# A transformer kernel on one core: order of norms, evictions and first units at three places, and a layer norm split five to three

## What is computed

```
h = h + rms_norm(first_block_output, post_norm_gain)
# layer 1, gated MLP
u, v, z = split(rms_norm(h, a_pre_g) @ w_in, 3)        # 3 x 2048 columns
u = gelu(u);  v = layer_norm(gelu(v), ln_g, ln_b)
s = causal(w_s) mixed over the 128 tokens of a chunk of v, + b_s
y = (u * s * silu(z)) @ w_out
h = h + rms_norm(y, a_post_g)
# layer 2, windowed attention
k, v = rms_norm(h, kv_norm_g) @ w_k, ... @ w_v         # 256 columns each
q, z = rms_norm(h, b_pre_g) @ b_w_in ...
```

## Time and profile before

| | |
|---|---|
| median of 3 runs | 2735.89 us (2731.44 to 2737.82) |
| profiled execution, its own time | 2731.15 us |
| its span in the profile | 2729.3 us |
| PE busy | 2634.8 us, 97% of the span |
| DVE, ACT, POOL busy | 1319.5, 819.5, 1039.3 us |
| mean granted TensorE clock | 0.991 |

### The profile page before, as it was taken

How to read it: one execution, slowest core, us unless ns; L and a number is a source line. 1 busy time by engine, 2 the same in 40 slices (tenths; PEclk the granted TensorE clock), 3 DMA queues, 4 the chain that set the end, 5 groups by cost and what they waited for, 6 DMA issues and landing times.

```text
span 2729.3 us, 42831 instructions
## 1 busy us (share of the span) xinstructions
PE 2634.8 (97%) x17184; PEld 2150.5 (79%) x17184; DVE 1319.5 (48%) x2475; ACT 819.5 (30%) x1623; POOL 1039.3 (38%) x1310
## 2 busy tenths in 40 slices
PE   6999999999999999999899899999999998999999
PEld 5778787777877878787787788788887887877777
DVE  4225343445857667585533533543435006477643
ACT  3344343536214131321213311211113103455531
POOL 2322332323233132321367433344444555444452
PEclk9999999999999999999999999999999998999999
DMA  4111111111101010111432211111111113111122
GB/s 134 41 38 47 51 40 51 47 39 46 49 24 59 21 47 27 34 48 63 158 124 77 78 39 47 39 47 47 42 44 47 47 51 96 39 47 40 47 109 85
DMA packets 203989, 153.92 MB, mean 56 GB/s; under 512 B 5264, under 2 KB 183824, under 8 KB 203280
## 3 DMA queue, kind: packets, MB, share of 16 engines
q1 hardware_dynamic: 186256, 106.44, 13.2%
q10 hardware_dynamic: 17536, 44.74, 4.4%
HBM read 128.10 MB, written 23.07 MB: 55 GB/s over the span
## 4 chain that ended last, share of the span: by engine, by line
PE 78%; DVE 14%; ACT 6%; issue 1%; DMA 1%; POOL 1%; DVEq 0%; ACTq 0%; SPq 0%; POOLq 0%
PE gemm L621 19%; PE gemm L623 19%; PE gemm L622 19%; ACT prob L2377 3%; DVE neg_logits L1804 2%; DVE prob L1819 2%; PE scores L672 1%; PE weighted L699 1%; PE scores L869 1%; PE probs_t L684 1%; PE probs_t L866 1%; PE scores L1044 1%; PE scores L858 1%; PE probs_t L887 1%; DVE stats L1808 1%
## 5 line engine op out<-in xcount | busy, mean ns | idle before, releaser
L582 POOL CAST w_hi<-w_raw 128x512 fp32r<-128x512 f32 x346 | 240.5, 695 | 1570.1 <-PE gemm L623 1504.0
L621 PE MATMUL gemm<-h_hi,w_hi 128*128 128x512 f32 x1904 | 779.3, 409 | 10.9 <-ACT q_t L2021 7.6
L623 PE MATMUL gemm<-h_hi,w_lo 128*128 128x512 f32 x1904 | 746.9, 392 | 0.0
L622 PE MATMUL gemm<-h_lo,w_hi 128*128 128x512 f32 x1904 | 745.4, 391 | 0.0
L584 POOL TENSOR_TENSOR w_lo<-w_raw,w_hi 128x256 fp32r<-128x256 f32 x692 | 590.7, 854 | 54.7
L621 PEld LDWEIGHTS gemm<-h_hi,w_hi 128*128 128x128 f32 x1904 | 360.0, 189 | 90.4 <-issue 22.5
L623 PEld LDWEIGHTS gemm<-h_hi,w_lo 128*128 128x128 f32 x1904 | 358.9, 189 | 78.3
L622 PEld LDWEIGHTS gemm<-h_lo,w_hi 128*128 128x128 f32 x1904 | 360.3, 189 | 65.2 <-issue 1.9
L1586 DVE TENSOR_TENSOR scaled_product<-gemm,norm_rstd 128x512 f32<-128x512 f32 x108 | 74.7, 691 | 310.7 <-PE gemm L623 308.6
L1284 DVE CUSTOM_DVE_ANT_0 neg_logits<-scores,bias_tile 128x128 f32<-128x128 f32 (+1 forms) x192 | 67.6, 352 | 148.7 <-PE scores L672 142.9
L621 PE MATMUL gemm<-xn_hi,w_hi 128*128 128x512 f32 x288 | 116.9, 406 | 2.6 <-DVE xn_lo L1732 2.2
(11 more groups left out here) (511 smaller groups left out, 4528.7 us busy)
## 6 DMA issues: line engine op xcount, KB each, us to landing
w_raw<-in_w_in SPq DMA_DIRECT2D x73, 512.0 KB, 3.9
w_raw<-in_a_w_in SPq DMA_DIRECT2D x48, 512.0 KB, 3.8
gates_scratch<-o_f ACTq DMA_DIRECT2D x32, 256.0 KB, 2.0
merge_gates<-gates_scratch ACTq DMA_DIRECT2D x4, 2048.0 KB, 15.0
w_raw<-in_a_w_out SPq DMA_DIRECT2D x16, 512.0 KB, 3.8
w_raw<-in_b_w_in SPq DMA_DIRECT2D x16, 512.0 KB, 3.9
x_rows<-in_x SPq DMA_DIRECT2D x8, 512.0 KB, 8.3
w_raw<-in_w_out SPq DMA_DIRECT2D x8, 512.0 KB, 3.9
```

Source lines behind the costliest of these rows:

```text
L582: Q(pool.tensor_copy(weight_part(u, 0, ks), raw[:, s, ks, :]))
L621: pe.matmul(dst, w_high, hi(k, h), start=first, stop=False)
L622: pe.matmul(dst, w_high, lo(k, h), start=False, stop=False)
L623: m = pe.matmul(dst, w_low, hi(k, h), start=False, stop=last)
```

## The change

At place A, `v_pair` runs the first three steps of V0 before the first of V1, and then goes on in pairs. The sum for the first block's second half moves from after step 2 to after step 4, and the spread of that norm from the end of the pair to after step 5. `v_next` puts its sum one step earlier for half 0 and two steps earlier (before all of V2) for half 1, and the spread one step earlier. DVE takes two evictions one tile earlier, and the statistics of group 1 (four `bn_stats`) go behind the evictions of group 2. The transposition of `w_s` comes one V unit later.

At place B, DVE normalises five chunks and ACT three. DVE empties the first half of Z0 after its second chunk, and the second half after its fifth. PE computes the first half of U1 before it waits for the layer norm.

At place C, the second norm of the residual is worked out one tile earlier and spread one step earlier. The first norm of half 1 comes one tile later on DVE and ACT. The first half of V1 is emptied one tile earlier. K0 of half 1 runs its first three steps before K1's first.

```diff
             def v_pair(h):
-                for k in range(KT):
+                for i in range(2):
+                    for k in range(3):
+                        h2_ready(k, h)
+                        gemm_step(U_V + i, h, k, *H2)
+                for k in range(3, KT):
                     h2_ready(k, h)
                     for i in range(2):
                         gemm_step(U_V + i, h, k, *H2)
-                    if (h, k) == (0, 2):
+                    if (h, k) == (0, 4):
                         sum_half(1, O_SECOND[-1], ADD_OUT[1, O_SECOND[-2]], SQ_OUT[1, O_SECOND[-1]])
-                if h == 0:
-                    spread_cols(4, 8)
+                    if (h, k) == (0, 5):
+                        spread_cols(4, 8)
             def v_next(h):
                 for k in range(KT):
+                    if k == 1 - h:
+                        sum_half(h, KT - 1, ADD_X2[h, KT - 2], SQ_X2[h, KT - 1])
                     gemm_step(U_V + 2, h, k, *H2)
-                    if k == 1:
-                        sum_half(h, KT - 1, ADD_X2[h, KT - 2], SQ_X2[h, KT - 1])
-                    if k == 4:
+                    if k == 3:
                         spread_cols(4 * h, 4 * h + 4)
...
-                if g == 5:
+                if g == 6:
                     pe.wait_ge(E("ws_in"), 32)
...
                 for h in range(2):
-                    if i or h:
+                    if (i, h) not in ((0, 0), (1, 0)):
                         gemm_half(U_UZ + 2 * i, h, *H2)
                 for h in range(2):
                     gemm_half(U_UZ + 2 * i + 1, h, *H2)
-                pe.wait_ge(E("v_normed"), 4)
-                pe.wait_ge(E("v_normed_act"), 4)
+                if i == 0:
+                    gemm_half(U_UZ + 2, 0, *H2)
+                pe.wait_ge(E("v_normed"), 5)
+                pe.wait_ge(E("v_normed_act"), 3)
...
-                if k == 6:
+                if k == 5:
                     spread_cols(4, 8)
...
+            def second_ready(k, h):
                 pe.wait_ge(E("low_part"), PART["xn"] + KT + k + 1)
+            for j in range(2):
+                for k in range(3):
+                    second_ready(k, 1)
+                    gemm_step(U_KV + j, 1, k, *XN)
+            for k in range(3, KT):
+                second_ready(k, 1)
                 for j in range(2):
                     gemm_step(U_KV + j, 1, k, *XN)
...
                 if k == 4:
-                    v_scaled(1, 0)
-                if k == 5:
                     v_scaled(1, 1)
+                if k == 5:
                     v_rows_in(0)
...
             for b in range(2):
                 v_scaled(2, b)
+            v_stats(1)
             for b in range(2):
                 v_scaled(3, b)
...
-            for n in range(4):
+            for n in range(5):
                 V(v.tensor_scalar(vln[:, n, :], vln[:, n, :], mv[:, n, 0:1], stat[:, 336 + n:337 + n], ALU.subtract, ALU.mult), E("v_normed"))
-            evict_z(0)
+                if n == 1:
+                    scaled(U_UZ + 1, 0, scaled_g[:, 0, :])
+            scaled(U_UZ + 1, 1, scaled_g[:, 1, :])
...
-                if k == 6:
+                if k == 5:
                     rstd(4, 8, MB)
...
-                if k == 0:
+                if k == 1:
                     rstd(0, 4)
-                if k == 1:
+                if k == 2:
                     rstd_in_sbuf(3)
                     for j in range(2):
                         key_part(j, 0)
                 if k == 3:
                     value_part(0, 0)
-                if k == 5:
+                if k == 4:
                     value_part(1, 0)
...
-                    for n in range(4, 8):
+                    for n in range(5, 8):
                         A(a.activation(vln[:, n, :], vln[:, n, :], ACT.Identity, bias=stat[:, 344 + n:345 + n], scale=stat[:, 336 + n:337 + n]), E("v_normed_act"))
...
-                if k == 7:
+                if k == 6:
                     root(4, 8)
...
-                if k == 1:
+                if k == 2:
                     root(0, 4, (0, 4))
```

More of the change, by code:

```diff
@@ L1631, in v_rows_in, with v_stats @@
                       E("vln_rows"))
+                if g != 1:
+                    v_stats(g)
+            def v_stats(g):
                 if g in (1, 3) or g % 4 == 3:
@@ L1635, in v_rows_in @@
                         V(v.bn_stats(bn[:, n, s, :], vln[:, n, HALF * s:HALF * s + HALF]))
-                if g == 4:
+                if g == 5:
                     dve.wait_ge(E("ws_tr"), 1)
@@ L1656, in _ @@
                     v_scaled(0, 1)
+                if k == 3:
+                    v_scaled(1, 0)
                 if k == 4:
-                    v_scaled(1, 0)
+                    v_scaled(1, 1)
                 if k == 5:
-                    v_scaled(1, 1)
                     v_rows_in(0)
```

## The result

The changed kernel took 2713.66 us in the median of four runs (2712.95 to 2719.32), the kernel before 2735.22 us (2731.44 to 2737.82). The ratio is 0.9925, interval 0.9911 to 0.9939. The profiled execution has a span of 2711.1 us against 2729.3, so 18.2 us are gone in it; the forecast had 20.5.

The account below looks back on a forecast made before the run. PE bounds the kernel, so only its waits and slow-clock stretches at three places count. Gains of 8.4 + 5.2 + 6.9 = 20.5 us from the 2735.89 us median give 2715 us, range 2708 to 2724.

Parts of the forecast that it names:

- The three waits named: PE's waits: 6.4 us for DVE's evictions at A, 3.7 us for ACT at B, 5.6 us for a V half's eviction at C.
- Place A, 8.4 us: Place A, V3's end and its transposition: 9.3 us earlier, taken as 8.4 us, with ends at 5.5 and 10.5 us.
- the mild slowing of POOL: Place A: POOL's split of V2 loses 1 us beside DVE's work, not the 2.5 us of the strict port rule.
- I add 2 us: Place A, from V2's start: 2 us added to PE's 1533.2 for starting behind a 4.4 us wait and a sum, giving 1535.2.
- slow stretch of 1.7 us: Place A: a further stretch at low clock, 1.7 us with half a chance, lowering the gain from 9.3 to 8.4 us.
- Place B, 5.2 us: Place B: U1's first half fills PE's wait for the layer norm, gaining 5.2 us, or 3.5 us with a slow stretch.
- cover of half a us for U1's bank: First MLP round: DVE empties U1's first half, needed by Z1, half a us ahead of PE; the thinnest cover.
- Place C, 6.9 us: Place C: the transposition comes at 2317.9 against 2324.76, 6.9 us earlier, with ends at 5 and 7.5 us.
- DVE leads by 3.0 us: Place C: the earlier spread gains DVE 1.8 us and filling its stall for half 0's sum 1.2 us.
- (1): Place A gains only 0 to 5 us, by POOL's slowing and low clock; the whole 12 to 17 us, about 2721; chance 0.14.
- (2): C's 5.6 us wait becomes another of equal length, A gives 0, B alone stays: 5 us, about 2731; chance 0.05.
- (3): The 16 MLP rounds become bound by DVE, evictions late in each, from 1.6 us a round on: 2742; chance 0.02.

Follow-up runs that it names:

- the second measurement of the same kernel: The changed kernel, unaltered, run again beside the kernels with one place's edits each: 2718.0 us, ratio 0.9938 to the kernel before.
- the two kernels above: The changed kernel with the layer norm split four to four again: 2718.0 us; the changed kernel without U1's first half ahead of the wait: 2722.1 us.
- with filler in both: 14 matmuls of unread product added at place C: on the changed kernel 2715.3 us, on the kernel before 2734.4 us, on that with A's edits alone 2730.3 us.
- B alone: Only place B's edits, on the kernel before: 2730.0 us, ratio 0.9985.
- the kernel with both fillers: The changed kernel with place A's half-0 sum ahead of V2, plus unread matmuls, 8 at place A and 14 at place C: 2709.7 us, ratio 0.9902.

## Why the prediction held, and where it did not

**Bounds and waits.** The three waits named were the ones that went, and what followed each place only moved. That reading carried the forecast. Of the signs named, two came out differently: the longest wait for a low part at place C is 1.7 us, not about 1, and the new wait at A is 2.5 us, not about 4. The total fits better than its parts: 20.5 us forecast and 20.5 us by the first ratio, but 17.0 us by the second measurement of the same kernel, 18.2 us in the profile, and 14.5 us for the three places measured singly. That the number was met so closely is partly luck.

**Place A, 8.4 us: 8.7 in the profile.** V2's start, the mild slowing of POOL and the end of V3's wait in half 1 came as written. I had put the new wait at 4.4 us; it was 2.5 us here, since a slow stretch delayed PE ahead of it, and 4.1 us where none did. V2 began at 18.3 us in both cases. The 8.7 us are those of a good execution. Of the seven profiles with this order at A, three took 61.0 to 61.2 us and four 64.0 to 64.2, a gain of 5.5 to 5.8 us, near my lower end of 5.5. In the four nothing slow lies ahead of V2, but 10.2 us of slow time begin at V2 itself, the sum is made in it, and DVE waits 7.20 us for it instead of 4.18 (the changed kernel once more, PE's row and DVE's):

```profile
1510.88 0.79 PE L621 MATMUL max_rows<-h_hi,w_extra_v 128*128 128x512 f32 x1 [4.12 <-POOL w_extra_v L584]
```

```profile
1515.84 0.16 DVE L1580 TENSOR_SCALAR stats<-weighted 128x4 f32<-128x4 f32 x1 [7.20 <-PE weighted L925]
```

So the mis-sized term here is "I add 2 us" together with the slow stretch of 1.7 us "with half a chance": the four show it about 3 us too small. Over all runs A's edits alone gave 3.8 us (1.4 to 6.6), which leaves the 8.4 us outside.

**Place B, 5.2 us: 5.6.** The slow stretch behind the old wait also slowed the products after the 16 small matmuls (0.77 us for the first one in before, 0.48 now), which I had not counted. The cover of half a us for U1's bank was right: the eviction ended at 1731.7 and PE needed it at 1732.3. What I did not say is that the fill does it all; the two kernels above show it.

**Place C, 6.9 us: 4.3, under my lower end of 5.** The mis-sized step is "DVE leads by 3.0 us". Its mechanism is right at full clock: there the last low part begins 3.4 us early (before's 2318.76, less 15.18 us by which the place began earlier, against the row below), the new order takes 55.8 us, 7.1 us less than the 62.9 of before, and with filler in both it is 7.2 to 7.8 us (63.6 and 64.2 to 56.4, with 6.8 us of slow time left in the old order).

```profile
2300.22 0.69 DVE L1754 TENSOR_TENSOR xn_lo<-block2a_out,xn_hi 128x512 fp32r<-128x512 f32 x1
```

What I left out is that the sum which DVE waits for is PE's own, made in a stretch in which PE waits for low parts and its clock falls in most executions. At half clock the sum comes late, DVE's wait is 3.18 instead of 0.83 us, and the lead is gone. My lower end of 5 us took a slow stretch by what PE loses in it, or half the lead gone; here only 0.5 of the 3.0 us was left. This is the account of two profiles. Over all runs C's edits alone gave 6.6 us (4.1 to 9.0), near the 6.9; where the slow time lies in before's other runs was not seen, their granted clock over the whole kernel goes down to 0.988, against 0.991 in the profiled one.

**The rivals.** (1), little from A by POOL or by the clock: in part, in the executions with 5.8 us at A and by the clock, not by POOL; the second measurement of the whole, 17.0 us, lies on its upper edge. (2) did not occur. (3) did not: the stretch from the second round to place C is the same within 0.1 us in all profiles.

**What is not settled.** Some slow stretches come back at nearly the same distance from V0's first step (the second of place A 37.9 us behind it both in before and in B alone), so a fixed shift may meet good or bad points again and again. Whether that explains the small total of A's edits (0.14%, with and without filler at C, where the place shrinks by 5.6 to 8.7 us in the profiles) is open: each kernel was seen in one profile only, the changed one in two.

## What to carry to other kernels

A stage in which PE waits for another engine's tiles, and that engine for a sum of PE's, has several lengths, by how much slow clock falls into it and where (place C's new order: 55.8 to 62.9 us). The result of a reordering there cannot be read from a single profile. Compare many runs, or stages with the same slow time, or fill the waits with matmuls. And if a wait for weights is to come anyway, the small sum that starts the next chain can stand ahead of it: that took away DVE's wait of 4.18 us here.

## What was unexpected of the hardware

Matmuls that compute nothing made the kernel with both fillers steadier and not measurably slower: eight of them, 2.1 us, in a wait of 2.5 us, and fourteen beside waits for low parts, left no slow time in two stretches that had had 3.4 to 10.2 us of it (A, new order) and up to 20.5 us (C). Without them the new order of place C took 55.8, 58.6, 60.8 or 62.9 us, depending on 0, 6.8, 10.2 or 20.5 us at 1.2 GHz.
